# Reordering the operand hand-over of the output projection, and moving every seventh low part from VectorE to GpSimd

## The reference, cut to what matters

```python
def odd_layer(x, norm_g, w_in, conv_w, w_out):
    h = rmsnorm_2(x, norm_g)
    z = h @ w_in                                  # the 56 "pairs" 0..55 of the kernel
    ...                                           # dilated attention y_c, gated convolution y_d
    return x + jnp.concatenate([y_c, y_d], axis=-1) @ w_out   # pairs 56..63: 1024x2048 by 2048x1024
...
return rmsnorm_2(h, final_norm)
```

## Time and profile before

| | |
|---|---|
| median of 3 runs | 3244.09 us |
| the profiled execution | 3243.6 us, span 3241.9 us |
| TensorE matmul busy | 3104.1 us (96% of the span) |
| VectorE / ScalarE / GpSimd busy | 1707.5 / 1452.3 / 1683.6 us |
| GpSimd low parts of quarters, L3002, 128 x 512 | 1455 ns each in the mean |

### The profile page before, as it was taken

One profiled execution on the slowest core, in us unless ns is written; L12 is line 12 of the kernel. 1 busy time (PEld: TensorE's weight loads), 2 busy tenths in 40 slices (PEclk: granted clock), 3 DMA queues, 4 the chain that ended last, 5 costly groups with the idle time before them and its releaser, 6 DMA issues. The chain is left out here.

```text
span 3241.9 us, 43876 instructions
## 1 busy us (share of the span) xinstructions
PE 3104.1 (96%) x16242; PEld 2572.7 (79%) x16242; DVE 1707.5 (53%) x2457; ACT 1452.3 (45%) x2457; POOL 1683.6 (52%) x1096
## 2 busy tenths in 40 slices
PE   6989999889899989999999999999999999999998
PEld 4777887866788868788888788888888888888777
DVE  5366633854799876622523744444444444467544
ACT  5156313723677743333401555445455445333443
POOL 2331323042322249976643656556556556689886
PEclk8999999999899989999999999999999999999999
DMA  8230212173999952222432111111111111244553
GB/s 297 56 86 21 57 40 75 44 260 119 337 400 394 375 166 69 78 98 62 155 101 80 40 47 52 46 53 46 46 56 43 47 56 43 89 146 162 169 173 106
DMA packets 341492, 388.12 MB, mean 120 GB/s; under 512 B 29367, under 2 KB 297563, under 8 KB 335012
## 3 DMA queue, kind: packets, MB, share of 16 engines
q1 hardware_dynamic: 329374, 344.39, 31.7%
q0 software_dynamic: 4896, 16.78, 2.0%
q10 hardware_dynamic: 7014, 24.17, 1.9%
HBM read 313.73 MB, written 68.16 MB: 118 GB/s over the span
## 5 line engine op out<-in xcount | busy, mean ns | idle before, releaser
L3002 POOL TENSOR_TENSOR quarter_lo<-quarter_w_sums,quarter_hi 128x512 fp32r<-128x512 f32 x325 | 470.5, 1455 | 244.5 <-ACT quarter_hi L2996 242.1
L3002 POOL TENSOR_TENSOR quarter_lo<-quarter_raw,quarter_hi 128x512 fp32r<-128x512 f32 x244 | 355.0, 1455 | 280.2 <-ACT quarter_hi L2996 273.2
L3092 PE MATMUL odd_z<-odd_t_hi,quarter_hi 128*128 128x512 f32 x876 | 362.4, 414 | 4.3 <-POOL quarter_lo L3002 3.8
L2996 ACT CAST quarter_hi<-quarter_w_sums 128x512 fp32r<-128x512 f32 x325 | 202.4, 623 | 362.9 <-PE first_z L3094 172.5
L3092 PE MATMUL first_z<-odd_t_hi,quarter_hi 128*128 128x512 f32 x868 | 358.8, 413 | 6.1 <-issue 4.8
L3094 PE MATMUL odd_z<-odd_t_hi,quarter_lo 128*128 128x512 f32 x876 | 343.6, 392 | 0.0
L3093 PE MATMUL odd_z<-odd_t_lo,quarter_hi 128*128 128x512 f32 x876 | 342.1, 391 | 0.0
L3094 PE MATMUL first_z<-odd_t_hi,quarter_lo 128*128 128x512 f32 x868 | 339.8, 391 | 0.0
L3093 PE MATMUL first_z<-odd_t_lo,quarter_hi 128*128 128x512 f32 x868 | 338.3, 390 | 0.0
L2996 ACT CAST quarter_hi<-quarter_raw 128x512 fp32r<-128x512 f32 x244 | 151.5, 621 | 120.7 <-PE first_z L3094 55.8
L276 POOL TENSOR_TENSOR w_hi<-w_raw,zero_col 128x1024 fp32r<-128x1024 f32 x25 | 49.7, 1990 | 288.1 <-DMA w_raw<-in_w_in 98.0
(11 more groups left out here) (716 smaller groups left out, 7790.2 us busy)
## 6 DMA issues: line engine op xcount, KB each, us to landing
quarter_raw<-in_odd_w_in SPq DMA_DIRECT2D x224, 256.0 KB, 3.5
raw_gate<-in_w_gate SPq DMA_DIRECT2D x16, 2048.0 KB, 15.7
raw_up<-in_w_up SPq DMA_DIRECT2D x16, 2048.0 KB, 15.8
raw_down<-in_w_down SPq DMA_DIRECT2D x16, 2048.0 KB, 15.5
quarter_raw<-in_even_w_in SPq DMA_DIRECT2D x64, 256.0 KB, 3.3
start_w_mod<-in_w_mod SPq DMA_DIRECT2D x11, 1024.0 KB, 10.8
w_raw<-in_w_in SPq DMA_DIRECT2D x16, 512.0 KB, 3.8
mix_w_early<-in_w_mod SPq DMA_DIRECT2D x8, 1024.0 KB, 12.0
```

What stands on the lines that cost most here:

```text
L2996: act.copy(self.home(n)[0][:], self.source(m, i)).then_inc(self.hi_done, 1)
L3002: pool.tensor_tensor(lo[:], self.source(m, i), hi[:].bitcast(F32), ALU.subtract).then_inc(self.split, 1)
L3092: pe.matmul(to, w_hi[:, kt], t_hi[:, kt], start=(begins and kt == 0), stop=False, skip_group_check=True)
```

## The change

Four things change, all around the two places where the streamed operands change.

- SyncE: `load_operand(chunk, 5)` is issued before the first part of the next pair's quarters.
- ScalarE: `operand_hi(chunk, 0)` stands ahead of `copy(m, 2)` of the last pair before the chunk, and the others follow one each behind `hi(m, 2)` to `hi(m, 5)`. In chunk 0, `operand_hi(0, 5)` stands ahead of `copy(56, 0)` and `operand_hi(0, 6)` behind `copy(56, 1)`; in chunk 1 numbers 5 and 6 stand ahead of and behind `hi(60, 0)`.
- GpSimd makes the low part of operand 6, after all the quarter work of the chunk's first pair. VectorE no longer does.
- VectorE: `operand_lo(chunk, i)` stands ahead of the join that it stood behind; in pairs 61 to 63 `add(m, 2)` stands ahead of `mean`.

```diff
@@ SyncE (and the same with load_operand(1, 5) and m + 5)
                     for i in range(5):
                         load_operand(0, i)
+                    load_operand(0, 5)
                     load(m + 1, (0,))
-                    load_operand(0, 5)
                     load_operand(0, 6)
@@ GpSimd
                     for m in range(1, PAIRS + OUT_PAIRS):
                         quarters.pool(pool, m)
+                        if m in (PAIRS, PAIRS + CHUNK_PAIRS):
+                            chunk = place(m)[0]
+                            pool.wait_ge(operand_hi_done, 7 * chunk + 7)
+                            pool.wait_ge(operand_split, 7 * chunk + 6)
+                            pool.tensor_tensor(odd_tokens[6][1][:], odd_sums[6][:], odd_tokens[6][0][:].bitcast(F32), ALU.subtract).then_inc(operand_split, 1)
@@ ScalarE, pair 55 (pair 59 is changed in the same way, with operand_hi(1, ...))
                         copy(m, 1)
                         hi(m, 1)
+                        if c == KT - 1:
+                            operand_hi(0, 0)
                         copy(m, 2)
-                        hi(m, 2)
-                        for i in (3, 4, 5):
+                        for i in (2, 3, 4, 5):
+                            hi(m, i)
                             if c == KT - 1:
-                                operand_hi(0, i - 3)
-                            hi(m, i)
-                        if c == KT - 1:
-                            operand_hi(0, 3)
+                                operand_hi(0, i - 1)
                         copy(m, 6)
                         hi(m, 6)
@@ ScalarE, pair 56
+                    operand_hi(0, 5)
                     copy(m, 0)
                     hi(m, 0)
-                    operand_hi(0, 4)
                     copy(m, 1)
+                    operand_hi(0, 6)
+                    copy(m, 2)
                     hi(m, 1)
-                    operand_hi(0, 5)
-                    copy(m, 2)
                     hi(m, 2)
-                    operand_hi(0, 6)
@@ ScalarE, pair 60
-                    for i in range(7):
-                        if i < 3:
-                            operand_hi(1, i + 4)
+                    operand_hi(1, 5)
+                    hi(m, 0)
+                    operand_hi(1, 6)
+                    for i in range(1, 7):
                         hi(m, i)
@@ VectorE, pairs 53, 55 (split only in 55); pair 59 likewise
-                            join(m, 3)
+                            for i in (3, 4, 5):
+                                if split:
+                                    operand_lo(0, i - 3)
+                                join(m, i)
                             if split:
-                                operand_lo(0, 0)
-                            join(m, 4)
-...
                                 operand_lo(0, 3)
@@ VectorE, pairs 56 and 60: operand_lo(., 6) goes
                     join(m, 3)
-                    operand_lo(0, 6)
...
                     add(m, 1)
+                    operand_lo(1, 5)
                     add(m, 2)
-                    operand_lo(1, 5)
-                    operand_lo(1, 6)
@@ VectorE, pairs 61 to 63
                         add(m, 1)
+                        add(m, 2)
                         mean(2 * q + 2, js)
                         ...
-                        add(m, 2)
                         inverse(q + 1, js)
```

More of the change, by code:

```diff
@@ L4206, in _ @@
                         load_operand(1, i)
+                    load_operand(1, 5)
                     load(m + 5, (0,))
-                    load_operand(1, 5)
                     load_operand(1, 6)
@@ L4629, in _ @@
                         hi(m, 1)
+                        if last:
+                            operand_hi(1, 0)
                         copy(m, 2)
-                        hi(m, 2)
-                        for i in (3, 4, 5):
+                        for i in (2, 3, 4, 5):
+                            hi(m, i)
                             if last:
[L4634 to L4637, removed]
+                                operand_hi(1, i - 1)
                         copy(m, 6)
@@ L5018, in _ @@
                             add_x(2 * turned)
+                        if last:
+                            operand_lo(1, 0)
                         join(m, 3)
                         if last:
-                            operand_lo(1, 0)
+                            operand_lo(1, 1)
                         join(m, 4)
-                        if last:
-                            operand_lo(1, 1)
                         if turned is not None:
                             add_x(2 * turned + 1)
+                        if last:
+                            operand_lo(1, 2)
                         join(m, 5)
                         if last:
-                            operand_lo(1, 2)
                             operand_lo(1, 3)
```

## The result

The changed kernel takes 3259.93 us (median of 5 runs, 3256.16 to 3260.74) against 3243.22 us for the kernel before on the same chip: 16.7 us more. The forecast was 3258.5 us.

The account below looks back on a forecast made before the run. Time could be won or lost only where TensorE idles, with GpSimd's chain ending last in both places. 8.4 + 5.0 + 1.2 = + 14.6 us on 3243.6, plus 0.5 to the median: 3258.5 us forecast, range 3250 to 3265.

Parts of the forecast that it names:

- The early cast decides: ScalarE, pairs 55 and 59: operand 0's cast waits ahead of the copy; (55,4) idles 2.85 us, (59,4) 1.4 us.
- The turns: GpSimd and VectorE alternate before (56,0): five GpSimd turns of 1.2 us, four VectorE of 2.15; (56,0) 9.7 us later.
- GpSimd's operation: Operand 6's low part on GpSimd takes 4.8 us (4.7 to 5.2), ahead of 5.3 us of work before (57,0).
- The second place: Around pairs 59 to 61: (60,0) 4.15 us late, (61,0) at 3177.5 in place of 3172.50, + 5.0 us.
- The clock: TensorE after new idle in the first place: one more low-clock spell, 1.7 us, of which + 1.2 counted; bounds 0 and 4.
- the first place: Around pairs 55 to 57: (57,0) starts at 3094.4 in place of 3086.02, + 8.4 us.
- Costed at nothing: the joins: VectorE's low parts ahead of joins: 0 us, since a join's bank is wanted a pair later; if late, 0.69 us.
- Costed at nothing: the rest: Operand 5's earlier load, `add(m,2)` ahead of `mean` and GpSimd's added sync waits: hidden or within slack, 0 us.
- (a): Rival, both places: late GpSimd loses no more turns to VectorE, only the shift costs, + 3.2 and + 3.3; 3250 us; chance 0.12.
- (b): Rival, ScalarE's early cast: operand 0 has landed when asked for, so not slower; 3247 us, within noise; chance 0.08.
- (c): Rival: GpSimd's long operation also blocks VectorE; two or three low-clock spells add 4 to 6 us; 3263 us; chance 0.12.

Follow-up runs that it names:

- one SBUF input: Changed kernel, but VectorE's low parts of operands 0 to 5 subtract old PSUM content in four 128x512 operations, leaving out the true low part: 3247.63 us, ratio 1.0016.

## Why the prediction was right, point by point

- *The early cast decides.* Right in kind. (55,4) idled 2.31 us (2.85 forecast; the operand landed 5.4 us after its issue, not 5.7), (59,4) 1.43 us (1.4 forecast), and GpSimd stood idle 4.36 us. Undoing it takes 11.4 us of 16.7 away.
- *The turns.* Right for the changed kernel, and (56,0) came 9.0 us late, 9.7 forecast. But the prediction puts them down to the cast; with the cast alone two of them are not there, and (56,0) is 5.2 us late. The low part for (56,0) ended at 3070.06; the forecast, moved by the 0.43 us that this execution was ahead, says 3070.8. With one SBUF input the turns and the delay vanish.
- *GpSimd's operation.* 4.61 us against 4.8. The Trainium skill's figure (GPSIMD Engine Reference, Elementwise — side-by-side cycle accounting), 4.497 us, was 0.1 short. (57,0) came 8.8 us late, forecast 8.4 (its own steps, 3088.8 and 5.3, make 3094.1 and not 3094.4) and 1.2 for the clock.
- *The second place.* (60,0) was 4.4 us later from (59,3), forecast 4.15, but (61,0) 6.1, forecast 5.0. The missing 1.1 us lies between them, in the term that held operand 6's load and the low parts (60,4) to (60,6): (60,0) itself ran at the lower clock, so the high part for (60,4) came late, and operand 6 (issued at 3164.89) kept ScalarE waiting 1.72 us; its cast could start 7.5 us after the issue. The forecast had no such wait.
- *The clock.* The term was one more spell. There were four against one. Only the one behind (57,0) shows as time, 1.6 us; those at (55,4) and (56,0) lie beside GpSimd's chain, that at (60,0) is part of the 1.1 us, and the old one behind (61,0) went, which gives the 1.6 back. Outside the two places the term of + 1.2 came to nothing.
- *The sum.* + 14.9 us in the profile against + 14.6. That they meet so closely is luck in part: the first place was 0.4 over, the second 1.1 over, and the clock 1.2 under. In the medians it is + 16.7, and no profile shows the other 1.8. With 0.5 us from the profiled execution to the median the forecast should also have read 3258.7, not 3258.5.
- *Costed at nothing: the joins.* Wrong in its reason and, with the early cast, probably in its price. I wrote that the join's bank is wanted a pair later; (m,6) waits for join (m,4) of its own pair, and the price was 3.4 us of idle and not 0.69. The idle stayed hidden, in the changed kernel because (55,4) was late already, and without that because GpSimd sets (57,0). What the prediction priced within the turns is the other effect: with the low parts ahead of the joins VectorE does not stand still behind the late (55,4), and GpSimd meets it twice more, the 3.8 us at (56,0) between the early cast alone and the kernel with GpSimd's part undone.
- *Costed at nothing: the rest.* All of it together, with the joins, costs + 1.3 us with zero in its interval when the two other edits are undone. SyncE's order, the other casts' places and `add(m, 2)` were not tried one by one.
- *Rivals.* (a) falls with the five slow operations of GpSimd, (b) with the 4.06 us wait for operand 0, which in no profile here could be cast earlier than 5.2 us after its issue. (c), more spells at the low clock, came in part: four spells, but at most 1.1 us of net cost, not 4 to 6.

Open: why the early cast alone costs 10.9 us in the medians and 7.8 in its profile; its own profiled execution was 5.5 us under its median. Its (55,3) started at 3045.30, 2.6 to 6.7 us earlier than in the other profiles, so most of that lies ahead of the change, and one profile cannot say what the other executions spent behind it.

## What to carry to other kernels

Before an instruction is moved ahead in an in-order queue, look up when its own input lands: here one cast, moved ahead of two short instructions, waited 4 us and held up TensorE and GpSimd through them. Where two engines exclude each other, a shift can cost more than itself, if the delayed one meets more of the other's turns: 9.0 us at (56,0) in the changed kernel, but 5.2 with the cast alone, where the other engine was held up as well. And edits that are harmless or small each by itself should be tried together, place by place: totals that add up do not show that the parts do. Idle time of TensorE is only lost where the chain behind it has no other late link: 3.4 us of new idle cost nothing, while taking work off the engine at the end of the chain gave 5 us only after the join that had then become late was moved too.

## What the runs showed of the hardware

A VectorE subtraction of 128x2048 with both inputs in SBUF held GpSimd's 512-element operations up to 3.1 to 3.3 us each; the same in four instructions of 128x512 with one input in PSUM left them at 1.30 us and took 2.47 us itself. GpSimd's 128x2048 subtraction took 4.56 to 4.62 us, 3.6 times its 512-element one (1.29 us). A spell at the lower of TensorE's two clocks (matmuls 0.43 us apart) came behind single idles of 2.31, 6.05, 2.22 and 5.43 us in the changed kernel, but not behind the one of 2.10 us before (61,0). Behind 3.1 us of idle before (60,0) the granted clock was 1.00 in the kernel before and 0.50 for 6.1 us in the one with GpSimd's part alone, so a single idle does not tell. Operand 0, 1 MB, could be cast 5.2 to 7.8 us after its issue.
